# Prompt attention of a hybrid decoder step: the first products of the paged compression as three single-pass products of split operands, low parts of the pages by GpSimd

## What is computed

```python
seg = rows[:, :n_seg * CMP_STRIDE].reshape(B, n_seg, CMP_STRIDE, 2, A_KV, A_DH)
w1r = w1.reshape(2, 2, CMP_STRIDE, A_DH, CMP_HID)
per = jnp.einsum('bnjcgd,cxjdh->bnxcgh', seg, w1r)
hid = per[:, :-1, 0] + per[:, 1:, 1] + bias[:, None, :]
```

## Time and profile before

| | |
|---|---|
| runs without profile | 2049.57 us median of 3 (2047.11 to 2049.88) |
| profiled execution | span 2054.4 us, mean granted TensorE clock 0.979; no separate time is given for it |
| busy, share of the span | PE 96%, PEld 83%, DVE 41%, ACT 35%, POOL 7% |
| prompt attention | some 942 to 1236 us, TensorE bounds it |
| products of L1355 in this stage | 576 records, two per product |

### The profile page before, as it was taken

How to read it: one execution, slowest core, us unless ns; L and a number is a source line. 1 busy time by engine, 2 the same in 40 slices (tenths; PEclk the granted TensorE clock), 3 DMA queues, 4 the chain that set the end, 5 groups by cost and what they waited for, 6 DMA issues and landing times. The chain is left out here.

```text
span 2054.4 us, 37910 instructions
## 1 busy us (share of the span) xinstructions
PE 1972.4 (96%) x14895; PEld 1702.9 (83%) x14895; DVE 851.9 (41%) x1717; ACT 718.1 (35%) x1434; POOL 137.8 (7%) x266
## 2 busy tenths in 40 slices
PE   7999999999999989998999998999998999999998
PEld 7999999999999956576666665666655899999998
DVE  7232325523333254444454443555555522243332
ACT  6332223333233223332555453434333411142322
POOL 0000000000000021110000001122211011100000
PEclk9999999999999999888999998999999999999999
DMA  5552233333334234434444447988887622223320
GB/s 185 176 188 95 75 103 106 106 100 98 103 106 111 86 134 157 178 113 148 141 134 145 152 155 278 326 291 327 323 314 262 219 83 83 89 90 116 116 70 24
DMA packets 153140, 313.65 MB, mean 153 GB/s; under 512 B 16894, under 2 KB 66687, under 8 KB 149507
## 3 DMA queue, kind: packets, MB, share of 16 engines
q1 hardware_dynamic: 139848, 272.95, 39.9%
q0 software_dynamic: 11520, 37.76, 5.0%
q10 hardware_dynamic: 1594, 0.53, 0.1%
HBM read 279.44 MB, written 40.00 MB: 155 GB/s over the span
## 5 line engine op out<-in xcount | busy, mean ns | idle before, releaser
L261 PE MATMUL mm<-x_hi,w_hi 128*128 128x288 f32 x1696 | 368.2, 299 | 14.2 <-DVE w_lo L393 14.2
L261 PE MATMUL mm<-x_hi,w_lo 128*128 128x288 f32 x1696 | 363.9, 296 | 0.0
L261 PE MATMUL mm<-x_lo,w_hi 128*128 128x288 f32 x1696 | 363.6, 296 | 0.0
L393 DVE TENSOR_TENSOR w_lo<-region,w_hi 128x1024 fp32r<-128x1024 f32 x106 | 129.8, 1225 | 381.0 <-ACT w_hi L292 381.0
L261 PEld LDWEIGHTS mm<-x_hi,w_hi 128*128 128x128 f32 x1696 | 274.5, 189 | 15.8 <-issue 12.5
L261 PEld LDWEIGHTS mm<-x_hi,w_lo 128*128 128x128 f32 x1696 | 273.9, 189 | 0.0
L261 PEld LDWEIGHTS mm<-x_lo,w_hi 128*128 128x128 f32 x1696 | 273.7, 189 | 0.0
L292 ACT ACTIVATE w_hi<-region 128x1024 fp32r<-128x1024 f32 x106 | 112.0, 1057 | 339.3 <-PE mm L261 339.2
L2240 PE MATMUL o_mm<-o_feat_hi,o_w_hi 128*128 128x288 f32 x1024 | 219.5, 296 | 0.3 <-DVE o_feat_lo L2397 0.3
L2240 PE MATMUL o_mm<-o_feat_lo,o_w_hi 128*128 128x288 f32 x1024 | 219.3, 296 | 0.0
L2240 PE MATMUL o_mm<-o_feat_hi,o_w_lo 128*128 128x288 f32 x1024 | 219.3, 296 | 0.0
(11 more groups left out here) (461 smaller groups left out, 2490.4 us busy)
## 6 DMA issues: line engine op xcount, KB each, us to landing
wide<-pages SPq DMA_DIRECT2D x256, 256.0 KB, 4.9
region<-w_in SPq DMA_DIRECT2D x106, 512.0 KB, 3.9
s_kv<-pages POOLq DMA_DIRECT2D x128, 256.0 KB, 7.5
s_kv<-pages SPq DMA_DIRECT2D x128, 256.0 KB, 7.2
m_state<-state SPq DMA_DIRECT2D x4, 2056.0 KB, 11.4
s_wnd<-win_pages SPq DMA_DIRECT2D x8, 1024.0 KB, 9.9
wide<-w_out SPq DMA_DIRECT2D x8, 1024.0 KB, 8.9
o_w_raw<-w_out SPq DMA_DIRECT2D x8, 1024.0 KB, 7.6
```

Source lines behind the costliest of these rows:

```text
L261: last = nc.tensor.matmul(mm[:, s % 3, y, 0:HALF], w[:, m % RING, kk, :], f[:, k, y * HALF:(y + 1) * HALF], start=k == 0 and i == 0, stop= ...
L393: v.tensor_tensor(wlo[:, m % RING], raw[:, m % RING], whi[:, m % RING].bitcast(F32), ALU.subtract).then_inc(wlo_done, 1)
```

## The change

The 288 products of the 18 units in prompt attention are made from split operands in the type fp32r, which TensorE takes in one pass: high part of weight by high part of page, high by low, low by high. The high part is a copy that rounds (ACT), the low part the difference (weights: DVE, once; pages: POOL). A piece is a quarter of a half-unit, 512 columns: 144 pieces. High parts of pages have four buffers laid over space that is free in this stage; the low parts lie over the pages' own area further on. ACT now waits for a unit's landing, not TensorE, and each piece passes ACT, POOL, TensorE. Each duo on TensorE makes two pieces (12 products) in place of four steps; ACT makes the two high parts of duo d+1 between `copied(d - 1)` and the exponentials of duo d+1. At the start, TensorE's 32 steps become 16 pieces, with ACT's order written out and the weights' low parts ahead of the compressed softmax on DVE. The maximum of duo 0 moves behind both `compressed_prob`. POOL's DMAs move in between its subtractions, an output store to duo d % 8 == 3. Later stages keep `hidden_step`.

```diff
+def pages_high(nc, act, B, piece):
+    half_unit, y = divmod(piece, 4)
+    u, x = divmod(half_unit, 2)
+    if x + y == 0:
+        act.wait_ge(B.comp_in[u % 2], 16 * UP * (u // 2 + 1))
+    if half_unit >= 1:
+        if y == 3:
+            act.wait_ge(B.h_done, half_unit)
+        else:
+            act.wait_ge(B.piece_done, 3 * (half_unit - 1) + y + 1)
+    nc.scalar.activation(B.page_hi[y].rearrange("p k n c -> p n k c"), part_of(B.comp, piece), ACT.Copy).then_inc(B.page_high, 1)
+def pages_low(nc, pool, B, piece):
+    pool.wait_ge(B.page_high, piece + 1)
+    nc.gpsimd.tensor_tensor(part_of(B.comp_lo, piece), part_of(B.comp, piece), B.page_hi[piece % 4].bitcast(F32).rearrange("p k n c -> p n k c"),
+                            ALU.subtract).then_inc(B.page_low, 1)
+def hidden_pieces(nc, pe, B, pH, piece):
+    half_unit, y = divmod(piece, 4)
+    u, x = divmod(half_unit, 2)
+    if y == 0 and half_unit >= len(pH):
+        pe.wait_ge(B.h_split, half_unit + 1 - len(pH))
+    pe.wait_ge(B.page_low, piece + 1)
+    low = part_of(B.comp_lo, piece)
+    for k in range(2):
+        high = B.page_hi[y][:, k]
+        for i, (w, f) in enumerate(((B.cw1_hi, high), (B.cw1_hi, low[:, :, k]), (B.cw1_lo, high))):
+            last = nc.tensor.matmul(pH[half_unit % len(pH)][:], w[x][:, 2 * y + k, :], f, start=y + k + i == 0, stop=y == 3 and k == 1 and i == 2)
+    last.then_inc(B.h_done if y == 3 else B.piece_done, 1)
...
-    STEPS, LATE = 4, 16
+    PIECES, LATE = 2, 16
...
-            for f in range(NF):
-                if f < NF - 1:
+            for k in range(16):
+                pages_low(nc, pool, B, k)
+            for d in range(ND):
+                for k in range(PIECES):
+                    pages_low(nc, pool, B, 16 + PIECES * d + k)
+                if d % 8 == 3 and d >= 11:
+                    f = d // 8 - 1
                     pool.wait_ge(out_ready, f + 1)
                     pool.dma_start(B.cat_dram[8 + f, :, 0:TP], cat[:, f % 2, :]).then_inc(stored[f % 2], 16)
-                if f + NAZ < NF:
-                    gate(f + NAZ)
+                    if f + NAZ < NF:
+                        gate(f + NAZ)
...
-                for k in range(STEPS):
-                    hidden_step(nc, pe, B, pH, 32 + STEPS * d + k)
+                for k in range(PIECES):
+                    hidden_pieces(nc, pe, B, pH, 16 + PIECES * d + k)
...
-            for g in range(2):
-                compressed_exp(g)
-            for g in range(2):
-                for x in range(2):
-                    hidden_split(nc, act, B, pH, 2 * g + x)
-                compressed_copied(g)
+            s_.activation(B.cw1_hi[0], B.cw1[:, 0], ACT.Copy).then_inc(cw_high, 1)
+            high(0, 4)
+            s_.activation(B.cw1_hi[1], B.cw1[:, 1], ACT.Copy).then_inc(cw_high, 1)
+            high(4, 6)
+            compressed_exp(0)
+            high(6, 7)
+            hidden_split(nc, act, B, pH, 0)
+            high(7, 8)
+            compressed_exp(1)
+            high(8, 11)
+            hidden_split(nc, act, B, pH, 1)
+            high(11, 12)
+            compressed_copied(0)
+            high(12, 15)
+            hidden_split(nc, act, B, pH, 2)
+            high(15, 16)
+            hidden_split(nc, act, B, pH, 3)
+            compressed_copied(1)
...
+                if d == 0:
+                    high(16, 16 + PIECES)
                 if d >= 2 and d % 2 == 0:
                     hidden_split(nc, act, B, pH, 4 + d // 2 - 1)
                 if d >= 1:
                     copied(d - 1)
+                if d + 1 < ND:
+                    high(16 + PIECES * (d + 1), 16 + PIECES * (d + 2))
...
+            def weights_low(x):
+                dve.wait_ge(cw_high, x + 1)
+                v.tensor_tensor(B.cw1_lo[x], B.cw1[:, x], B.cw1_hi[x].bitcast(F32), ALU.subtract).then_inc(cw_low, 1)
```

More of the change, by code:

```diff
@@ L1358, in hidden_step, with part_of @@
         last.then_inc(B.h_done, 1)
+def part_of(comp, piece):
+    half_unit, y = divmod(piece, 4)
+    u, x = divmod(half_unit, 2)
+    slot = (u % 2) * UP
+    return comp[:, slot:slot + UP, :].rearrange("p n (k x c) -> p n k x c", k=8, x=2)[:, :, 2 * y:2 * y + 2, x, :]
+def pages_high(nc, act, B, piece):
[14 more added lines that the diff above has]
+def hidden_pieces(nc, pe, B, pH, piece):
+    half_unit, y = divmod(piece, 4)
+    u, x = divmod(half_unit, 2)
+    if y == 0 and half_unit >= len(pH):
[7 more added lines that the diff above has]
+    last.then_inc(B.h_done if y == 3 else B.piece_done, 1)
 def hidden_split(nc, act, B, pH, half_unit):
@@ L1400, in attend_prompt @@
         pH = [ps("a_pH", [P, UC])]
+        over = lambda n, s, at: nc.alloc_sbuf_tensor_at(n, s, F32R, offset=at)[:]
+        tail_at = B.wide_at + 4 * (2 * UP * CH + 5 * KV * PAST // SEG)
+        B.comp_lo = over("a_comp_lo", [P, 2 * UP, CH], B.wide_at)
+        B.cw1_hi = [over(f"a_cw1_hi{x}", [P, 8, P], tail_at + 4 * 8 * P * x) for x in range(2)]
+        B.cw1_lo = [over("a_cw1_lo0", [P, 8, P], B.land_at + 4 * 16 * TP), sb("a_cw1_lo1", [P, 8, P], F32R)[:]]
+        B.page_hi = [over(f"a_page_hi{i}", [P, 2, UP, 32], at) for i, at in enumerate((
+            tail_at + 4 * 16 * P, tail_at + 4 * 20 * P, B.land_at + 4 * 8 * TP, B.newmask_at))]
+        B.page_high, B.page_low, B.piece_done = sem("a_page_high"), sem("a_page_low"), sem("a_piece_done")
+        cw_high, cw_low = sem("a_cw_high"), sem("a_cw_low")
         az_in, stored = [sem(f"a_az_in{i}") for i in range(NAZ)], B.cat_stored
@@ L1502, in _ @@
             scores(1)
+            pe.wait_ge(cw_low, 1)
             for g in range(2):
-                for k in range(16):
-                    hidden_step(nc, pe, B, pH, 16 * g + k)
+                for k in range(8):
+                    if k == 4:
+                        pe.wait_ge(cw_low, 2)
+                    hidden_pieces(nc, pe, B, pH, 8 * g + k)
                 compressed_turned(g)
@@ L1546, in compressed_copied, with high @@
                 s_.activation(pcT[:, g, :], pT[:, g % 2, :], ACT.Copy).then_inc(ct_ready, 1)
-            for g in range(2):
-                compressed_exp(g)
-            for g in range(2):
-                for x in range(2):
-                    hidden_split(nc, act, B, pH, 2 * g + x)
-                compressed_copied(g)
+            def high(first, last):
+                for k in range(first, last):
+                    pages_high(nc, act, B, k)
+            s_.activation(B.cw1_hi[0], B.cw1[:, 0], ACT.Copy).then_inc(cw_high, 1)
[16 more added lines that the diff above has]
+            compressed_copied(1)
             for d in range(ND):
@@ L1630, in _ @@
             step(v.memset(pc[:].rearrange("p g h n -> p (g h n)"), 0.0))
+            def weights_low(x):
+                dve.wait_ge(cw_high, x + 1)
+                v.tensor_tensor(B.cw1_lo[x], B.cw1[:, x], B.cw1_hi[x].bitcast(F32), ALU.subtract).then_inc(cw_low, 1)
             for g in range(2):
                 compressed_masked(g, 1)
-            for g in range(2):
-                compressed(g)
+            weights_low(0)
+            weights_low(1)
+            compressed(0)
+            compressed(1)
+            compressed_prob(0)
+            compressed_prob(1)
             maximum(0)
-            for g in range(2):
-                compressed_prob(g)
             hidden_added(nc, dve, B, 0)
@@ L2503, in step_kernel @@
             B.cmpmask = hold(prompt, "cmpmask", [P, 4, 32])
+            B.land_at = (nc.sbuf_base + 31) // 32 * 32
             land = hold(prompt, "landing", [P, KD * T])
```

2 lines of the change are left out of this document (added).

## The result

The changed kernel took 2052.09 us, the median of 16 runs (2048.7 to 2057.69), against 2046.39 us for the kernel before (16 runs, 2044.44 to 2049.88): a ratio of 1.0028, with an interval from 1.0021 to 1.0035. It is slower by 5.7 us, just outside the 0.2% named as the bound of no change. The three times of before that the prediction started from had a median 3.2 us above that of all 16.

The account below looks back on a forecast made before the run. The prediction took TensorE to bound the loop, with ScalarE and VectorE following. It added +4 us at the start and +3 in the loop to 2049.6, giving 2057 us, range 2042 to 2088.

Parts of the forecast that it names:

- The sum: Whole kernel: +4 us at the start and +3 in the steady loop make +7 on 2049.6, so 2057 us.
- Products: TensorE in the loop: single-pass products at 0.12 us each save 0.25 us per duo, 16 us over 64.
- High parts: ScalarE in the loop: two copies add 1.04 us per duo; groups take 15.7 against 15.88, leaving 2 to 3 of 16 us.
- the 32 us: ScalarE's waits for TensorE's products in the steady part before; their absence was a sign that the prediction was right.
- Low parts and the lock: GpSimd's 1.29 us low parts block VectorE's scalings through a shared port pair; steady part +3 us, between -3 and +13.
- The start: Before the loop, 16 pieces pass GpSimd in series, delaying the first turns: +4 us, bounds +0 to +8.
- Page loads: SP's loads, about 14 us a unit: slack about nothing, cost nothing while a group stays near 15.9 us, late next below that.
- A: Rival: the port pair does not block and ScalarE keeps up; 16 us realised less 2 at the start, 2035 us; chance 0.12.
- B: Rival: ScalarE's order binds the loop, the port hardly; 2044 to 2049 us; chance 0.19.
- C: Rival: the port pair becomes the bound, low parts lasting 1.5 to 1.6 us or blocks in twos; 2086 us; chance 0.20.
- D: Rival: TensorE's products run at 0.22 us each, as with 32 rows; 2107 us; chance 0.04.
- E: The forecast case: the loop at parity, the start late; 2051 to 2065 us; chance 0.45.

Follow-up runs that it names:

- experiment 11: Experiment 9's kernel, with SP also reading a unit's eight page numbers before its wait instead of behind it: 2039.0 us, 0.9957 of the kernel before.
- experiment 2: Changed kernel with each low part subtracting only 64 of 512 columns and the second product reading the high part again: 2042.4 us, 0.9979 of the kernel before.
- experiment 7: Changed kernel with VectorE's two scalings per duo also writing a column sum (accum_out), a form that doesn't wait for GpSimd: 2048.8 us, 1.0014 of the kernel before.
- experiment 9: Changed kernel with one high part moved ahead of ScalarE's split of the hidden products in even duos: 2045.5 us, 0.9996 of the kernel before.
- experiment 4: Changed kernel with both high and low parts cut to 64 of 512 columns, the second product reading the high part: 2031.2 us, 0.9928 of the kernel before.
- high_short: The kernel of experiment 3, the changed kernel with high parts cut to 64 of 512 columns from the fifth piece on: 2046.8 us.
- low_wait: The kernel of experiment 5, the changed kernel with GpSimd waiting between low parts: 2050.0 us.
- after: The changed kernel itself, with the whole change and no further edit, against the kernel before: 2052.09 us, ratio 1.0028.
- experiment 1: Changed kernel with the first two units of pages computed in full precision as in the kernel before: 2048.8 us, 1.0014 of the kernel before.
- experiment 3: Changed kernel with each high part from the fifth piece on rounding only 64 of 512 columns: 2046.8 us, 1.0001 of the kernel before.
- experiment 5: Changed kernel with GpSimd waiting before each low part until its previous one is written: 2050.0 us, 1.0022 of the kernel before.
- experiment 6: Changed kernel with each low part as two GpSimd instructions of 256 columns, without a wait between: 2051.7 us, 1.0034 of the kernel before.
- experiment 8: Changed kernel with the next duo's first high part before the copy of the turned probabilities, the second behind it: 2053.5 us, 1.0038 of the kernel before.

## Why the prediction was right, and where it wasn't

**The sum** was +7 on the runs shown, and the medians of all runs differ by 5.7. The time came out 4.9 under the forecast, 3.2 of which is the base. The verdict, slower by more than 0.2%, was that of the likeliest case. That the sum came so near is in part luck: the profiles give +5.1 for the start and -2.6 for the loop, and the rest of the 5.7 us lies in executions of which there is no profile.

**Products: right.** Their records start 0.12 us apart:

```profile
1124.31 0.28 PE L1401 MATMUL a_pH<-a_page_hi,a_cw_lo 128*128 128x256 f32 x1
1124.43 0.28 PE L1401 MATMUL a_pH<-a_page_hi,a_cw_hi 128*128 128x256 f32 x1
1124.55 0.29 PE L1401 MATMUL a_pH<-a_comp_lo,a_cw_hi 128*128 128x256 f32 x1
```

and the saving is 0.25 us per duo: experiment 11, in which nothing else is in TensorE's way, takes 127.02 - 119.15 = 7.87 us off 32 duos, 0.246 each. By the formula in the Trainium skill, "TensorE: Matmul & The Clock Gate", section "Back-to-back issue gap", which the page gives for an isolated product, it would have been 0.13 more. The trace doesn't show that.

**High parts: right in kind, a little too dear.** "ScalarE needs 3 x 3.4 = 10.2", 15.7 us for a group. The high parts last 0.629 us in the loop, 0.52 apart, as worked out, and ScalarE's order is the limit; but the groups take 15.0 and 15.85 us in turn, 15.5 on average against 15.9 before. Of 16 us it leaves 6.4 (3.22 for 32 duos), not 2 to 3. The working has a second error that hid part of this one. The four distances of the earlier trace rows add up to 15.44, the shorter of the two groups before (15.45 and 16.31), so the average lies 0.44 above them and not 0.2; with that the sum would have come to 15.97, no gain at all. ScalarE's 10.2 us for three duos was some 0.5 us too much. And ScalarE still waits 14.6 us for products in the 24 duos, where the absence of the 32 us was named as the sign.

**Low parts and the lock: the durations right, the loop wrong.** 1.29 us was predicted and 1.293 measured. The scalings rose, to 0.64 us in the mean and 1.82 at most, where 0.8 or more in the mean was named as the sign. The step that failed is "a block of one GpSimd operation makes 7.0, free; two make 8.33 ... I take +3", a price paid evenly by all duos. Experiments 2 and 7 take the lock away, and duos 24 to 55 don't move. What the profiles show of a cost are single waits of TensorE, up to 3.7 us, where a scaling meets a run of low parts or DMA issues without a gap. In the profiled execution of the changed kernel the longest, 2.3 us, stands in duos 20 to 23, where VectorE has the second half of the heads besides (one scaling of 1.82 and one of 1.45 us on end): these four take 19.61 us, against 17.68 and 17.74 in experiments 2 and 7. Not every wait there is the ports': in experiment 7 TensorE still waits 1.3 us for a scaling in duos 16 to 19. So from first turns to last the profiled loop won 2.6 us where +3 was predicted. The upper half of the runs lies 4 to 8 us above the profiled one, and the median 2.7; whether their loops are longer is open.

**The start: +5.1 in the profile, +4 predicted.** From the first high part:

```profile
946.08 2.19 ACT L1380 ACTIVATE a_page_hi<-wide 128x512 fp32r<-128x512 f32 x4 [9.56 <-DMA wide<-pages]
946.79 22.93 POOL L1386 TENSOR_TENSOR a_comp_lo<-wide,a_page_hi 128x512 fp32r<-128x512 f32 x16 [9.06 <-ACT a_page_hi L1380]
...
972.07 0.36 ACT L1637 ACTIVATE a_p<-a_pS,region 128x128 f32<-128x128 f32 x1
...
975.02 2.19 ACT L1380 ACTIVATE a_page_hi<-wide 128x512 fp32r<-128x512 f32 x4 [2.15 <-DMA wide<-pages]
...
979.84 0.63 PE L1523 MATMUL a_pT<-ident,a_p 128*128 128x128 f32 x2
```

The first exponential comes 26.0 us behind it, where 979 - 952.95 = 26.05 was predicted. The 16 low parts took 22.93 us against 16 x 1.29 = 20.6; a single one took up to 2.26 us beside VectorE's work, where the loop's median is 1.28. What was missed comes behind the exponential: 4.7 us to the first turns in the prediction, 7.8 in the trace. The pages of unit 2 weren't there (2.15 us). And the twelve products before the turns ran at the lower clock: 0.50 from 974.3 to 981.1, after TensorE had waited 1.7 us for exponentials up to 972.9, and with 3.1 us of waiting for the low part up to 977.15. They start 0.21 us apart and take 2.69 us, where twelve take 1.44 at 0.12.

**Page loads: "late next" was right, "cost to nothing" only for the loop.** They cost some 2 us in the start, and as soon as the order was mended they were the bound (experiment 9 against 11: 4.2 us of 32 duos, 6.5 in the median).

**The rivals.** A needed a pair that doesn't block and a ScalarE that keeps up: experiment 4 shows what that would bring, 2031 us rather than the 2035 given. B described the undisturbed loop, C and D didn't come: low parts stayed under 1.3, products at 0.12. The forecast E held by its start. Its "loop at parity" was not borne out: the profiled loop is shorter, and that the ports make up for it in the other executions is not shown.

## What to carry to other kernels

An engine that is half idle can still set the pace by its order: look in its timeline for an idle stretch with a train of work right behind it, and move what needn't wait into the stretch. When GpSimd takes over work beside VectorE's two-port operations, don't count blocked time by the mean; one blocked operation per iteration may be free, while a run of GpSimd's instructions without a gap, its DMA issues included, can hold VectorE for several of them. Look at the granted clock behind every long wait of TensorE. And when two limits lie close together, cut each alone and both: here 9.7 and 5.3 us made 20.9.

## What the runs showed of the hardware that was not expected

A VectorE scaling that waits for the ports isn't always served at the end of GpSimd's running instruction if the next follows at once: it waited up to 4.5 us, through four low parts (high_short). Mostly it is: of the 20 scalings over 0.9 us in the changed kernel, 16 ended within 0.25 us of the end of one low part although the next followed at once, and only one lasted through two. What decides between the two isn't shown. With a gap of about 0.1 us between low parts (low_wait) none of 33 waited for more than one; the longest of them was also held by DMA issues.

GpSimd's DMA issues (0.54 to 0.67 us each) can hold VectorE up too, though they seldom do. In the eight profiles in which GpSimd issued them in the loop beside whole or halved low parts (after, experiments 1, 3, 5, 6, 8, 9 and 11), 74 scalings began during an issue. 68 of them took 0.55 us or less, and six were held: 1.09, 2.37, 3.08, 3.51, 3.62 and 3.62 us. All of these but the one of 3.08 would have ended before the next low part began, had they taken 0.54 us.
